# A fused three-block network: the token-compression network of the second attention with its columns standing in TensorE, placed behind that attention's first scores, and bf16 filler products in the ends of the branches

## What is computed

```python
def compress_tokens(x, pe, w1, b1, w2, b2):      # for keys and for values
    xb = x[:, idx] + pe                          # 15 windows of 32 tokens, 64 values, 4 heads
    return jax.nn.gelu(xb @ w1 + b1) @ w2 + b2   # 2048 -> 256 -> 64

# nsa_mixer: 16 query heads in 4 groups
kcc, vcc = compress_tokens(kc, ...), compress_tokens(vc, ...)
o_cmp = attention(q, kcc, vcc)                   # 15 keys
o_sel = attention(q, ks, vs)                     # causal, all blocks selected at 256 tokens
o_win = attention(q, kw, vw)                     # causal window
o = g0 * o_cmp + g1 * o_sel + g2 * o_win
```

## Time and profile before

| | |
|---|---|
| runs | 1802.1, 1802.98, 1791.11 us (median 1802.1) |
| the profiled execution | 1789.85 us, of it the span 1787.6 us; mean granted clock 0.962 |
| PE busy | 1694.1 us, 95% of the span, 11348 matmuls |
| PEld, DVE, ACT, POOL busy | 85%, 68%, 51%, 32% |
| chain that ended last | PE 87%, DVE 5%, ACT 3%, DMA 3%, issue 2% |
| DMA | 341.14 MB, mean 191 GB/s |

### The profile page before, as it was taken

The page is one execution under the profiler, slowest core; times in us unless marked ns, Lnnn a source line. Parts: engine busy times, 40 slices in busy tenths (PEclk is TensorE's granted clock), DMA queues, the critical chain, the costliest instruction groups (busy, mean ns, idle before and its releaser), DMA issues.

```text
span 1787.6 us, 32466 instructions
## 1 busy us (share of the span) xinstructions
PE 1694.1 (95%) x11348; PEld 1520.5 (85%) x11348; DVE 1216.1 (68%) x2234; ACT 916.6 (51%) x1749; POOL 565.1 (32%) x230
## 2 busy tenths in 40 slices
PE   2997999999999999999999999989899999799998
PEld 1985899999999998788888878976799999589997
DVE  5467509779718993878887758639578877646665
ACT  2445444455469994454545454247544445554443
POOL 0780377989975455000000007320210004130000
PEclk8899899999999999999999999969999998989999
DMA  8665455556653335888888655343568764136663
GB/s 324 224 207 169 144 177 176 178 185 178 185 168 118 113 111 183 326 283 291 293 290 285 195 165 149 120 150 126 165 224 282 281 224 133 34 107 188 188 187 107
DMA packets 98568, 341.14 MB, mean 191 GB/s; under 512 B 12290, under 2 KB 16146, under 8 KB 98482
## 3 DMA queue, kind: packets, MB, share of 16 engines
q1 hardware_dynamic: 94130, 336.01, 56.9%
q10 hardware_dynamic: 4352, 4.02, 0.8%
HBM read 337.87 MB, written 1.07 MB: 190 GB/s over the span
## 4 chain that ended last, share of the span: by engine, by line
PE 87%; DVE 5%; ACT 3%; DMA 3%; issue 2%; ACTq 0%; SPq 0%; DVEq 0%
PE banks L611 25%; PE banks L612 25%; PE banks L613 25%; PE banks L890 3%; DMA arena<-in_ada 2%; DVE arena L1546 1%; PE banks L1054 1%; PE banks L776 1%; DMA ada_ring<-in_ada 1%; PE banks L750 1%; PE banks L682 1%; PE banks L789 1%; DVE arena L1653 1%; PE banks L675 1%; DVE negmax L1632 1%
## 5 line engine op out<-in xcount | busy, mean ns | idle before, releaser
L564 POOL TENSOR_TENSOR weights_low<-ring,weights_high 128x1024 fp32r<-128x1024 f32 x226 | 564.9, 2512 | 1041.1 <-DVE ht_low L1621 625.9
L1167 ACT ACTIVATE weights_high<-ring 128x1024 fp32r<-128x1024 f32 x480 | 505.2, 1054 | 510.1 <-PE banks L613 481.2
L611 PE MATMUL banks<-ht_high,weights_high 128*128 128x256 f32 x2008 | 582.5, 290 | 8.5 <-DVE ht_low L1621 6.0
L612 PE MATMUL banks<-ht_low,weights_high 128*128 128x256 f32 x2008 | 572.2, 285 | 0.0
L613 PE MATMUL banks<-ht_high,weights_low 128*128 128x256 f32 x2008 | 572.0, 285 | 0.0
L611 PEld LDWEIGHTS banks<-ht_high,weights_high 128*128 128x128 f32 x2008 | 389.5, 194 | 14.2 <-issue 11.4
L612 PEld LDWEIGHTS banks<-ht_low,weights_high 128*128 128x128 f32 x2008 | 389.7, 194 | 2.7
L613 PEld LDWEIGHTS banks<-ht_high,weights_low 128*128 128x128 f32 x2008 | 389.1, 194 | 0.0
L1601 DVE TENSOR_TENSOR weights_low<-ring,weights_high 128x1024 fp32r<-128x1024 f32 x254 | 310.5, 1223 | 40.2 <-ACT weights_high L1167 34.5
L611 PE MATMUL banks<-weights_high,ga_parts 128*128 128x512 f32 x504 | 197.7, 392 | 5.8 <-DVE ga_parts L1903 5.8
L612 PE MATMUL banks<-weights_low,ga_parts 128*128 128x512 f32 x504 | 197.0, 391 | 0.0
(11 more groups left out here) (249 smaller groups left out, 2328.8 us busy)
## 6 DMA issues: line engine op xcount, KB each, us to landing
ring<-in_stream SPq DMA_DIRECT2D x490, 512.0 KB, 3.6
arena<-in_ada SPq DMA_DIRECT2D x88, 512.0 KB, 4.1
ada_ring<-in_ada SPq DMA_DIRECT2D x56, 512.0 KB, 4.3
arena<-bias_rows ACTq DMA_DIRECT2D x1, 2048.0 KB, 13.4
X<-in_x SPq DMA_DIRECT2D x1, 1024.0 KB, 5.8
out<-X SPq DMA_DIRECT2D x4, 256.0 KB, 2.0
arena<-arena ACTq DMA_DIRECT2D x8, 127.5 KB, 4.9
arena<-in_norm_final SPq DMA_DIRECT2D x1, 512.0 KB, 4.6
```

The costliest lines, as they stand in the source:

```text
L564: pool.tensor_tensor(WL[:, c % SLOTS, :], ring[:, c % SLOTS, :], WH[:, c % HIGHS, :], ALU.subtract)\
L611: pe.matmul(out, wh, xh, start=start, stop=False, **kw)
L612: pe.matmul(out, wh, xl, start=False, stop=False, **kw)
L1167: act.activation(WH[:, c % HIGHS, :], ring[:, c % SLOTS, :], ACT.Copy).then_inc(S["high_ready"], 1)
```

## The change

1. **The compression network.** `WIN` is now the stationary operand (60 columns, "standing") and w1 the moving one, 256 columns at a time: 32 float32 products instead of 64. Keys go to rows 0 to 59 of bank 7 and values to rows 64 to 123, in turns. The bias b1 is added by two products with a row of ones; ACT applies GELU to two tiles of 60 x 256 (`HIDT`); four transposes turn them, and DVE copies the 240 columns to `HID`. The second layer is as before. w1 is laid out anew in memory (keys and values alternate), with the same bytes.
2. **Its place.** `nsa_v` goes to banks 6 and 7. `attention` takes functions to call beside its steps: the first layer (`phi_hidden`) behind the scores of steps 0 and 1, the transposes (`phi_turned`) behind step 0's, the second layer (`phi_out`) behind step 1's. ACT applies GELU at the start of its step 1 and copies the results in its step 2; DVE copies `HID` in its step 1. In group 0 the two `cmp` steps go last (sel, win, sel, win, cmp, cmp). Scores of `cmp` steps wait for ACT's copies. DVE finishes the gates behind the windows and not ahead of them.
3. **Loads and splits of `out2`.** SP issues the pieces of `ada` for the attention first, with one chunk of `out2` behind each of pieces 1 to 8. ACT's first four `high` of `out2` move from ahead of the attention to its steps 20 to 23, and POOL's `low` follow them.
4. **Fillers.** `keep_busy(n, bank)` issues n bf16 products of 128 x 512 whose result nobody reads. `ada_columns` issues two in each odd one of its eight blocks (8 a call, five calls); six more follow `norm_transpose` 1, 3, 4 and 5. The matmuls of the fillers are 64 in all.

```diff
-            return steps
+            steps.sort(key=order)
+            return [dict(s, n=step0 + i) for i, s in enumerate(steps)]
         att1 = plan(lambda g: ["moba" if g < 2 else "dsa"], 0, 0)
-        att2 = plan(lambda g: ["sel", "win", "cmp"], 8, 8)
+        att2 = plan(lambda g: ["sel", "win", "cmp"], 8, 8, lambda s: (s["g"], s["g"] == 0 and s["last"]))
...
-            load_chunks(ahead + SLOTS, chunk["out2"] + SLOTS)
+            load_chunks(ahead + SLOTS, chunk["out2"])
             ahead = chunk["out2"] + SLOTS
             for i in range(2 * DB):
                 load_ada(i, ADA_LAYER3, ADA_BEFORE["mixer2"] + i - 1 if i >= 2 else None, 12 * DB + i, "ada3_slot")
+                if 1 <= i <= SLOTS:
+                    load_chunk(chunk["out2"] + i - 1)
...
+            def keep_busy(n, bank):
+
+                for _ in range(n):
+                    pe.matmul(banks[:, bank, :], ident_b[:], const[:, 0:T].bitcast(BF16), start=True, stop=True)
+
             def ada_columns(accs, call):
 
                 n = len(accs)
                 for b in range(DB):
+                    if b % 2:
+                        keep_busy(2, 13 - SUM_BANK[call])
                     for v, acc in enumerate(accs):
...
+                if kind == "cmp":
+                    pe.wait_ge(S["cmp_taken"], 2)
...
                     scores(s, keys, queries)
+                if -1 in beside:
+                    beside[-1]()
                 for i, s in enumerate(steps):
                     if i + 2 < len(steps):
                         scores(steps[i + 2], keys, queries)
                     if i:
                         values(steps[i - 1], vals)
                     probs_transpose(s)
+                    if i in beside:
+                        beside[i]()
...
+            keep_busy(6, 13 - SUM_BANK[2])
...
             m.then_inc(S["gate_ready"], 1)
+            pe.wait_ge(S["out_taken"], OUTS["nsa"] + 16)
+            deep("nsa_v", 4, 512, per=2, bank=6)
+
+            def phi_hidden():
+                pe.wait_ge(S["windows_ready"], 4)
+                pe.wait_ge(S["phi_loaded"], 16 * 7)
+                pe.wait_ge(S["vv_taken"], 2)
+                for q in range(4):
+                    c = chunk["phi"] + 2 * q
+                    for kv in range(2):
+                        arrived(c + kv)
+                    for l in range(4):
+                        for kv in range(2):
+                            m = pe.matmul(banks[window_rows[kv], 7, 0:T], WIN[:, kv, 4 * q + l, :],
+                                          ring[:, (c + kv) % SLOTS, l * T:(l + 1) * T], start=q == 0 and l == 0, stop=False,
+                                          skip_group_check=True)
+                            if l == 3:
+                                m.then_inc(S["chunk_used"], 1)
+                pe.wait_ge(S["ones_row_ready"], 1)
+                for kv in range(2):
+                    m = pe.matmul(banks[window_rows[kv], 7, 0:T], ones_row[0:1, 0:60], A(A_B1R, 2, T)[0:1, kv, :],
+                                  start=False, stop=True, skip_group_check=True)
+                m.then_inc(S["phi_done"], 1)
+
+            def phi_turned():
+                pe.wait_ge(S["hid_ready"], 2)
+                for kv in range(2):
+                    r = window_rows[kv]
+                    if kv:
+                        pe.wait_ge(S["hid_turned"], 1)
+                    for mm in range(2):
+                        m = pe.transpose(banks[:, 7, T + (2 * kv + mm) * 60:T + (2 * kv + mm + 1) * 60],
+                                         HIDT[r, mm * P:(mm + 1) * P], ident[r, r])
+                    m.then_inc(S["hid_turned"], 1)
+
+            def phi_out():
+                pe.wait_ge(S["hid_taken"], 1)
+                for mm in range(2):
+                    m = pe.matmul(banks[:, 7, 0:60], A(A_W2D, 2, P)[:, mm, :], HID[:, mm, :], start=mm == 0, stop=mm == 1)
+                for g in range(4):
+                    o = banks[0:N_CMP, 7, T + g * HD:T + (g + 1) * HD]
+                    for mm in range(2):
+                        pe.matmul(o, HID[:, 2 + mm, g * N_CMP:(g + 1) * N_CMP], A(A_W2, 2, 2, HD)[:, 1, mm, :],
+                                  start=mm == 0, stop=False)
+                    m = pe.matmul(o, ones[0:1, 0:N_CMP], A(A_B2V, HD)[0:1, :], start=False, stop=True)
+                m.then_inc(S["cmp_ready"], 1)
             pe.wait_ge(S["rope_done"], ROPE2)
-            deep("nsa_v", 4, 512, per=2)
-
             pe.wait_ge(S["gate_taken"], 1)
-            for kv in range(2):
-                pe.wait_ge(S["windows_ready"], 2 * (kv + 1))
-                if kv == 0:
-                    pe.wait_ge(S["phi_loaded"], 16 * 7)
-                else:
-                    pe.wait_ge(S["hid_ready"], 2)
-                for q in range(4):
-                    c = chunk["phi"] + 4 * kv + q
-                    arrived(c)
-                    for l in range(4):
-                        l2 = 4 * q + l
-                        for mm in range(2):
-                            w = ring[:, c % SLOTS, (l * 2 + mm) * P:(l * 2 + mm + 1) * P]
-                            m = pe.matmul(banks[:, 2 + mm, 0:60], w, WIN[:, kv, l2, :], start=l2 == 0, stop=l2 == 15)
...
-            pe.wait_ge(S["cmp_taken"], 2)
-            pe.wait_ge(S["vv_taken"], 2)
-            pe.wait_ge(S["gates2_ready"], 1)
...
+            attention(att2, keys2, lambda s, h: Q2[:, h // 2, :], vals2, {-1: phi_hidden, 0: phi_turned, 1: phi_out})
...
+            keep_busy(6, 13 - SUM_BANK[6])
...
-            for kv in range(2):
-                act.wait_ge(S["chunk_used"], chunk["phi"] + 4 * (kv + 1))
-                for mm in range(2):
-                    act.activation(HID[:, 2 * kv + mm, :], banks[:, 2 + mm, 0:60], ACT.Gelu_apprx_tanh,
-                                   bias=A(A_B1, 4)[:, 2 * kv + mm:2 * kv + mm + 1]).then_inc(S["hid_ready"], 1)
...
+                act.activation(VV[:, t, :], banks[:, 6 + t, :], ACT.Copy).then_inc(S["vv_taken"], 1)
...
+            def take_hidden(i):
+                if i == 1:
+                    act.wait_ge(S["phi_done"], 1)
+                    for r in window_rows:
+                        act.activation(HIDT[r, :], banks[r, 7, 0:T], ACT.Gelu_apprx_tanh).then_inc(S["hid_ready"], 1)
+
+            def beside_att2(i):
+                if i == 2:
+                    act.wait_ge(S["cmp_ready"], 1)
+                    act.activation(A(A_KCC, 60), banks[:, 7, 0:60], ACT.Identity, bias=A(A_B2K, 1)).then_inc(S["cmp_taken"], 1)
+                    act.activation(A(A_VCC, T)[0:N_CMP, :], banks[0:N_CMP, 7, T:2 * T], ACT.Copy).then_inc(S["cmp_taken"], 1)
+                if i >= len(att2) - HIGHS:
+                    used(chunk["phi"] + 8 + i - len(att2))
+            attention(att2, take_hidden, beside_att2)
...
+                if step == 1:
+                    dve.wait_ge(S["hid_turned"], 2)
+                    dve.tensor_copy(A(A_HID, 240), banks[:, 7, T:T + 240]).then_inc(S["hid_taken"], 1)
```

58 lines of the change are left out of this document (23 added, 35 removed).

## The result

| | before | changed |
|---|---|---|
| median of 12 runs each (us) | 1794.82 (1790.12 to 1802.98) | 1783.89 (1775.99 to 1786.62) |
| ratio of the times | 1 | 0.9932, 95% interval 0.9917 to 0.9947 |
| profiled execution (us), its span | 1789.85, 1787.6 | 1781.73, 1779.9 |

The change brings 0.7%, 11 to 12 us (by the medians and by the ratio) of the 22.3 that the sum gave, and lies within the 1% that was to be told from nothing; 1777 was forecast. The two profiled executions stand 8 us apart.

The account below looks back on a forecast made before the run. PE was taken as the bound (87% of the chain), at half clock in the compression network and at branch ends. 21.8 - 3.5 + 4 = 22.3 us gained: 1767.5 from the profile, 1780 from the median; forecast 1777, range 1757 to 1797.

Parts of the forecast that it names:

- The network: Compression network moved into the second attention at full clock: 27.9 us against 49.7 up to step 6, 21.8 us gained.
- GELU to second layer: Network stretch from ACT's table load and GELU through the second layer and ACT's copies: 8.4 us.
- the row of the attention's values: Profile row used to cost the network's 32 products: 68 ns per 128-column record, doubled for 256 columns, 8.7 us.
- to step 6: Network's last stretch: ACT's exponentials, DVE's scaling and `ada` piece 4.5 us, then two `cmp` steps 3.8 us.
- The splits of `out2`: In attention steps 20 to 23, two of POOL's four `low` hold DVE, 1.73 us each: 3.5 us lost, bounds 0 and 7.
- The ends of branches: Fillers keep PE's clock up at five ends (column sums, transposes, next product): 4 us gained, full effect 6.3, lower bound -5.
- So the chunk ends at 1299.65 and not at 1301.4: 1.7 us: At end 3, the next product's first chunk runs as fast as DVE hands over `HTL`: 1.7 us gained.
- End 2 gives 1.6: At end 2, fillers (1.7 us) are outweighed by sums and transposes no longer at half clock: 1.6 us gained.
- rival 2: At the ends of branches the clock falls in spite of the fillers; price 4 + 4, 1785 us; chance 0.17.
- rival 3: At the attention's end all four `low` and the `high` lie on the path, plus a clock drop; 1784 us; chance 0.1.
- Rival 1: The network's first-layer products on different array halves do not overlap; price 5.4, 1782 us; chance 0.2.
- rival 4: Moved work doesn't lift the clock: PE stays at 1.2 GHz in network and five ends; 1822 us, slower; chance 0.04.

Follow-up runs that it names:

- the seven with the same code: Changed kernel and six follow-ups with its code unaltered from the second attention's first score to `out2`; that stretch took 87.4 to 93.4 us.
- e1: Changed kernel without any fillers; median 1778.1 us, ratio to the kernel before 0.9914.
- e5: Changed kernel without fillers and with the low parts of each MLP's third and fourth chunk on DVE, not POOL; median 1778.0 us, ratio to before 0.9919.
- e11: Changed kernel with the MLPs' two low parts on DVE and only the six fillers behind the transposes of ends 3, 4, 5; 1774.9 us, ratio to before 0.9900.
- e2: Kernel before with the fillers alone, at the same five ends; median 1794.5 us, ratio to before 1.0002.
- e12: Changed kernel with the network's first-layer keys and values on the same 60 array columns (timing only, wrong output); median 1784.3 us, ratio to before 0.9943.

## Why the prediction was right in its range and wrong in its middle

**The network** (21.8 us forecast, 18.8 in the profile, 18.8 to 21.4 in the seven with the same code). The mechanism held at each point: the scores before it took 2.0 us, the loads hid, full clock lasted to the end of the second layer. The table load lay under the products, which the sum had only as a possible 1.3 us more; this was spent elsewhere, since "GELU to second layer" took 8.2 us against 8.4 all the same. The products were put at 8.7 us by the row of the attention's values, 68 ns; they took 7.1. The Trainium skill ("TensorE: Matmul & The Clock Gate", Part 3, the mechanism) has small tiles in different column groups run concurrently, by which the prediction had worked out 7.1; the traces agree (7.12, and 14.02 on one half). The row was the worse guide: those products have 64 stationary and 128 moving columns, another form; why that form takes more than half of 110 ns wasn't tried. What was missing is the clock in "to step 6": the two `cmp` steps and their scores were costed at full clock, and ran at 0.62. That is the mis-sized term: 13.2 us against 4.5 + 3.8, 4.9 too little, of which the faster products hid 1.6. In e1, e5 and e11, where the clock was back sooner, the whole took 28.5 to 28.6, against 27.9 in the sum.

**The splits of `out2`** (3.5 forecast). 3.6 measured, and that the two agree is in part luck: only 2.0 us are the mechanism that was named, DVE beside POOL. The rest isn't a second hit on DVE, as the prediction had it, but half clock after PE's wait, 1.6 us. The Trainium skill ("SBUF — State Buffer", SBUF: two separate sides) says that one of the two engines holds the shared ports for the whole instruction; the trace agrees (a cast of 2.34 us that ends 0.15 behind POOL's split, 0.29 without one).

**The ends of branches** (4 gained forecast, at most 6.3, at worst 5 lost). This step failed. In the changed kernel's profile the five ends, with what follows them up to the next landmark, lose 5.9 (0.7 + 2.2 + 1.4 - 0.4 + 2.0); in e2, the fillers alone, they lose 4.4 in the profile and the timed runs gain nothing. Two of its sentences are wrong. "So the chunk ends at 1299.65 and not at 1301.4: 1.7 us" takes an earlier end of the first product for a gain without asking what is late next. Next is the first hidden tile: two splits of POOL begin up to 3 us behind the product's start and hold DVE, and PE gets its tile 8.7 us behind the product's start whether that product runs at half clock or at full. The prediction read this very rule at the earlier trace rows and applied it to the attention, not to the MLP that stands behind ends 3 and 5. And "End 2 gives 1.6" holds up to the product (1.9 in e2, with the clock up; the sums and row sums that it names give only 2.5 - 1.7 = 0.8, and the rest are the transposes of tile 1, 1.07 and not 1.95 us). It forgets what waits next: the rope, whose unit comes no earlier than DVE's modulation and POOL's splits allow, takes 2.4 us back. At end 4, 1.4 was forecast and 0.4 measured in the changed kernel, none in e2.

**The rivals.** The time came out at 1784, which is rival 2's and rival 3's number, by neither mechanism: at ends 3 and 5 the fillers did hold the clock or bring it back, against rival 2, and the splits cost 3.6 and not 7, against rival 3 (in e1, with the same code there, 6.8). Rival 1 (no overlap) is refuted by the 7.12 us and e12, rival 4 by PEclk 1.00 up to 1179. (The products that brought the clock back after 1300, which rival 4 gives 512 columns, have 256.) That three mechanisms gave 1782 to 1785 says how little the total tells of the cause. Of the 12.3 us that the first median stood above the profile, 5 were left in 12 runs (1794.82 against 1789.85), so a starting point of 1789 to 1795 would have been better than 1802. That 1777 is only 7 us off is therefore luck in part: 22.3 us from the true median would have been 1772.5, and half of the gain was missing. The range of 1757 to 1797 also holds the kernel before itself.

## What to carry to other kernels

Before a clock gain is booked, find who sets the start of the next stage but one; if that is a wait on another engine, the gain moves the half clock from a covered place to an open one, and the two edits (the fillers, and the splits off POOL) are worth more together than apart: at end 3 -1.4 and 0.6 us apart, 2.4 together. As far as these runs go, fillers belong right ahead of a dense stage (six of 512 columns did it alone), not into sums that another engine waits for and not into an attention step, where they didn't hold the clock. Products with 60 stationary columns should alternate between the halves of the array.
